# Sums of squares and roots of a query and key norm, with tokens on the partitions, and their order

## The reference

```
def rms_norm(x, g):
    xf = x.astype(jnp.float32)
    y = xf * lax.rsqrt(jnp.mean(xf * xf, axis=-1, keepdims=True) + NORM_EPS)
    return (y * g.astype(jnp.float32)).astype(x.dtype)
...
    q = q.reshape(B, T, H, 2, d)          # H = 4 heads, 2 components, d = 64
    k = k.reshape(B, T, H, 2, d)
    q = partial_rope(rms_norm(q, p['q_norm_g'])).astype(jnp.float32) * (d ** -0.5)
    k = partial_rope(rms_norm(k, p['k_norm_g'])).astype(jnp.float32)
```

## Time and profile before

| | |
|---|---|
| median of the runs | 2197.18 us |
| profiled execution, its own time | 2197.07 us |
| its span, first to last instruction | 2194.5 us |
| TensorE, matmuls | 1997.5 us (91%) |
| TensorE, weight loads | 1665.3 us (76%) |
| VectorE | 1411.1 us (64%) |
| ScalarE | 969.5 us (44%) |
| GpSimd | 349.1 us (16%) |
| granted TensorE clock, mean of the span | 0.950 |

### The profile page before, as it was taken

The page is one execution under the profiler, slowest core; times in us unless marked ns, Lnnn a source line. Parts: engine busy times, 40 slices in busy tenths (PEclk is TensorE's granted clock), DMA queues, the critical chain, the costliest instruction groups (busy, mean ns, idle before and its releaser), DMA issues. The chain is left out here.

```text
span 2194.5 us, 40752 instructions
## 1 busy us (share of the span) xinstructions
PE 1997.5 (91%) x16199; PEld 1665.3 (76%) x16199; DVE 1411.1 (64%) x2299; ACT 969.5 (44%) x1792; POOL 349.1 (16%) x354
## 2 busy tenths in 40 slices
PE   6999999997768888777999698899999999999999
PEld 4666777775545555576887387899999999988887
DVE  5877657674876667664777646656655565556666
ACT  7454467773744444443454322422232232333433
POOL 0000000000019993064454200000000000000000
PEclk8999999998879999958999899899999999999999
DMA  4111157777840001047884534022222222295343
GB/s 179 66 45 52 58 206 258 257 261 278 288 136 1 0 1 58 20 125 166 195 187 117 174 127 141 35 100 93 105 81 87 81 100 81 84 356 169 98 148 109
DMA packets 153305, 281.17 MB, mean 128 GB/s; under 512 B 13377, under 2 KB 85953, under 8 KB 150817
## 3 DMA queue, kind: packets, MB, share of 16 engines
q1 hardware_dynamic: 153120, 278.63, 39.8%
HBM read 172.53 MB, written 103.07 MB: 126 GB/s over the span
## 5 line engine op out<-in xcount | busy, mean ns | idle before, releaser
L2944 DVE TENSOR_TENSOR ff_lefts<-normed_raw,ff_lefts 128x512 fp32r<-128x512 f32 x154 | 105.5, 686 | 98.6 <-ACT ff_lefts L2828 98.6
L225 PE MATMUL ff_acc<-right_t_high,ff_lefts 128*128 128x320 f32 x528 | 163.1, 309 | 0.0
L224 PE MATMUL ff_acc<-right_t_low,ff_lefts 128*128 128x320 f32 x528 | 163.1, 309 | 0.0
L223 PE MATMUL ff_acc<-right_t_high,ff_lefts 128*128 128x320 f32 x528 | 163.1, 309 | 0.0
L223 PE MATMUL ff_acc<-normed_nl 128*128 128x512 f32 x385 | 149.8, 389 | 0.0
L225 PE MATMUL ff_acc<-normed_nl,normed_nh 128*128 128x512 f32 x385 | 149.8, 389 | 0.0
L2828 ACT CAST ff_lefts<-normed_raw 128x512 fp32r<-128x512 f32 x154 | 93.4, 620 | 116.2 <-DMA normed_raw<-in_w_up 56.1
L2854 ACT COPY normed_n<-ff_acc 128x640 f32<-128x640 f32 x66 | 45.9, 696 | 205.7 <-PE ff_acc L225 204.6
L1974 PE MATMUL at_pO<-heads_vt,at_amT 128*128 128x128 f32 (+1 forms) x624 | 104.6, 302 | 34.9 <-ACT at_amT L1918 24.5
L1974 PEld LDWEIGHTS at_pO<-heads_vt,at_amT 128*128 128x128 f32 (+1 forms) x624 | 82.8, 195 | 61.0 <-issue 40.0
L3016 DVE TENSOR_TENSOR normed_nl<-normed_raw,normed_nh 128x640 fp32r<-128x640 f32 x77 | 63.3, 822 | 91.7 <-ACT normed_nh L2877 91.7
(11 more groups left out here) (372 smaller groups left out, 5671.9 us busy)
## 6 DMA issues: line engine op xcount, KB each, us to landing
normed_raw<-dram_h SPq DMA_DIRECT2D x77, 320.0 KB, 3.0
ch_ops<-dram_sx SPq DMA_DIRECT2D x88, 256.0 KB, 5.2
dram_sx<-pr_sx SPq DMA_DIRECT2D x16, 1024.0 KB, 4.6
dram_h<-normed_spread_h SPq DMA_DIRECT2D x44, 320.0 KB, 2.3
pj_packed<-in_w_in SPq DMA_DIRECT2D x24, 512.0 KB, 4.9
heads_vt<-dram_ab SPq DMA_DIRECT2D x44, 256.0 KB, 5.4
normed_raw<-in_w_gate SPq DMA_DIRECT2D x22, 512.0 KB, 4.3
normed_raw<-in_w_up SPq DMA_DIRECT2D x22, 512.0 KB
```

Of the source, the lines that this page charges most:

```text
L223: nc.tensor.matmul(out, ll, rh, start=start, stop=False, skip_group_check=onto_kept)
L224: nc.tensor.matmul(out, lh, rl, start=False, stop=False, skip_group_check=onto_kept)
L225: return nc.tensor.matmul(out, lh, rh, start=False, stop=stop, skip_group_check=onto_kept)
L2944: tt(lefts[:, q % LEFTS, 1, :], raw[:, y, QUARTER[p], :], lefts[:, q % LEFTS, 0, :].bitcast(F32), ALU.subtract).then_inc(low, 1)
```

## The change

The sums are formed with the squares as weights: eleven blocks of 128 tokens, past each of which the two columns of `head_mean` move. The sums of token p of block w lie on partition p, columns 2w and 2w + 1: `st` is 128x22. ScalarE's root reads each of the 22 columns 64 times over (`by_rows`) and writes `rows`, 128x1408, tokens on the partitions. The spread takes each 128x128 block of `rows` as weights and the identity as the moving operand. `sq` is widened to 11 x 128 = 1408 columns, with the 96 at the end set to zero by GpSimd at the stage's start. `rows` has one buffer in place of two. The four `heads` matrices with their load, `quarter_mean` and the cuts at quarters and banks go.

The order changes too. TensorE does `sum_up(t+1)` ahead of `spread_roots(t)` and then the three `part`s; ScalarE does `root(t+1)` ahead of `square(t+2)`; VectorE does `inverse(t+1)` ahead of `scaled(t)`.

```
-        raw, sq0 = [g.raw_first, c.sb("raw1", (P, TOK))], c.sb("sq0", (P, TOK))
-        heads = c.sb("heads", (P, len(QUADS) * P))
+        raw, sq0 = [g.raw_first, c.sb("raw1", (P, TOK))], c.sb("sq0", (P, TT * P))
...
-        st = [c.sb(f"st{s}", (P, QTOK)) for s in range(2)]
-        rows = [c.sb(f"rows{s}", (P, QTOK)) for s in range(2)]
+        st = [c.sb(f"st{s}", (P, 2 * TT)) for s in range(2)]
+        rows = c.sb("rows", (P, TT * P))
...
-                sp.dma_start(heads[:, :], g.small_of("quarter_heads")).then_inc(small_in, 16)
...
             def _(pool):
+                for s in range(2):
+                    nc.gpsimd.memset(sq[s][:, TOK:TT * P], 0.0).then_inc(padded, 1)
                 sx_done(pool)
...
                     if t:
                         pe.wait_ge(meaned, t)
-                    for q, quad in enumerate(QUADS):
-                        last = nc.tensor.matmul(psq[quad, 0:QTOK], mean[:, :], sq[t % 2][:, q * QTOK:(q + 1) * QTOK], start=True, stop=True)
-                    last.then_inc(sums, 1)
+                    token_sums(nc, psq, sq[t % 2], mean[:, :]).then_inc(sums, 1)

                 def spread_roots(t):
                     pe.wait_ge(rooted, t + 1)
-                    if t == 0:
-                        pe.wait_ge(small_in, 16)
                     if t:
                         pe.wait_ge(roped, t)
-                    for lo, hi in zip(BANK_CUTS, BANK_CUTS[1:]):
-                        q = lo // QTOK
-                        last = nc.tensor.matmul(psn[:, lo:hi], heads[:, q * P:(q + 1) * P], rows[t % 2][:, lo - q * QTOK:hi - q * QTOK],
-                                                start=True, stop=True)
-                    last.then_inc(spreads, 1)
+                    spread(nc, psn, rows, ident, TOK).then_inc(spreads, 1)
...
                 for t in range(TILES - 1):
+                    sum_up(t + 1)
                     spread_roots(t)
-                    part(3 * t + 1)
-                    sum_up(t + 1)
-                    part(3 * t + 2)
-                    part(3 * t + 3)
+                    for n in range(3 * t + 1, 3 * t + 4):
+                        part(n)
...
                     act.wait_ge(inverted, t + 1)
-                    if t >= 2:
-                        act.wait_ge(spreads, t - 1)
-                    nc.scalar.activation(rows[t % 2][:, :], st[t % 2][:, :], ACT.Sqrt).then_inc(rooted, 1)
+                    if t:
+                        act.wait_ge(spreads, t)
+                    nc.scalar.activation(rows[:, :].rearrange("p (a n) -> p a n", n=HD), by_rows(st[t % 2][:, :], 2), ACT.Sqrt
+                                         ).then_inc(rooted, 1)
...
                     keep(3 * t + 1)
+                    root(t + 1)
                     if t + 2 < TILES:
                         square(t + 2)
-                    root(t + 1)
...
                 for t in range(TILES):
+                    if t + 1 < TILES:
+                        inverse(t + 1)
                     scaled(t)
                     if t + 1 < TILES:
                         with_sin(t + 1)
-                        inverse(t + 1)
                         with_cos(t + 1)
```

More of the change, by code:

```diff
@@ L87, in shape_constants @@
     out["centre"] = ((row[:, None] % HD == np.arange(HD)[None, :]) - 1 / HD).astype(np.float32)
[L88 to L92, removed]
     out["mean"] = np.full((P, 2), 1 / P, np.float32)
@@ L1006 @@
 QUADS = tuple(slice(BLK * q, BLK * (q + 1)) for q in range(P // BLK))
-QTOK = TOK // len(QUADS)
-BANK_CUTS = sorted({QTOK * q for q in range(len(QUADS) + 1)} | set(range(0, TOK, 512)))
 def steps_of(grp):
@@ L1528, in solve_and_attention_in @@
         two = lambda name, n=TOK: [c.sb(f"{name}{s}", (P, n)) for s in range(2)]
-        raw, sq0 = [g.raw_first, c.sb("raw1", (P, TOK))], c.sb("sq0", (P, TOK))
-        heads = c.sb("heads", (P, len(QUADS) * P))
-        mean, ident, swap, centre = (g.ahead_small[n] for n in ("quarter_mean", "ident", "swap", "centre"))
+        raw, sq0 = [g.raw_first, c.sb("raw1", (P, TOK))], c.sb("sq0", (P, TT * P))
+        mean, ident, swap, centre = (g.ahead_small[n] for n in ("head_mean", "ident", "swap", "centre"))
         swapped = c.sb("swapped", (P, 2))
-        st = [c.sb(f"st{s}", (P, QTOK)) for s in range(2)]
-        rows = [c.sb(f"rows{s}", (P, QTOK)) for s in range(2)]
+        st = [c.sb(f"st{s}", (P, 2 * TT)) for s in range(2)]
+        rows = c.sb("rows", (P, TT * P))
         swp = two("swp")
@@ L1538, in solve_and_attention_in @@
         cos, sin, v = g.cos_sb, g.sin_sb, g.v_rows
-        sq = [sq0, c.sb("sq1", (P, TOK))]
+        sq = [sq0, c.sb("sq1", (P, TT * P))]
         diag = [c.sb(f"diag{s}", (P, UNITS, BLK)) for s in range(2)]
@@ L1549, in solve_and_attention_in @@
             c.sem(n) for n in ("squared", "sums", "meaned", "rooted", "inverted", "spreads", "roped"))
-        small_in, blanked, swap_made, swap_kept = (
-            c.sem(n) for n in ("small_in", "blanked", "swap_made", "swap_kept"))
+        blanked, padded, swap_made, swap_kept = (c.sem(n) for n in ("blanked", "padded", "swap_made", "swap_kept"))
         sined, cosed, added = (c.sem(n) for n in ("sined", "cosed", "added"))
@@ L1725, in _ @@
                 pe.wait_ge(g.v_zeroed, 2)
+                pe.wait_ge(padded, 2)
                 turn_v(0)
@@ L1809, in inverse @@
                         dve.wait_ge(rooted, t - 1)
-                    nc.vector.tensor_scalar(st[t % 2][:, :], psq[:, 0:QTOK], 1e-6, None, ALU.add).then_inc(meaned, 1)
+                    nc.vector.tensor_scalar(st[t % 2][:, :], psq[:, 0:2 * TT], 1e-6, None, ALU.add).then_inc(meaned, 1)
                     dve.wait_ge(meaned, t + 1)
@@ L3108, in lend_ahead @@
         self.v_rows = [self.ahead.far(f"v{s}", (P, FT, 6 * CH)) for s in range(2)]
-        self.ahead_small = {n: self.ahead.far(n, (P, SCOLS[n][1])) for n in ("quarter_mean", "ident", "swap", "centre")}
+        self.ahead_small = {n: self.ahead.far(n, (P, SCOLS[n][1])) for n in ("head_mean", "ident", "swap", "centre")}
     def small_of(self, name):
```

## The result

The changed kernel takes 2235.3 us (median of 4 runs, 2231.06 to 2239.66) against 2194.31 before (median of 4 runs again, one of them the slow 3291.36 and the others 2189.88 to 2197.18): ratio 1.0188, 95% interval 1.0168 to 1.0208, 41 us slower. Forecast were 2226 and a range up to 2235. The direction, the ring and the size per tile came out. The forecast time is short by some 9 us and the forecast change, 28.8 us, by 12; the median lies 0.3 us above the range.

What follows compares the result with a forecast made beforehand. One stage was read as a ring of 10.5 us a tile, VectorE working through nearly all of it. A later first spread, six tiles of 15.0 us and a last round gave +28.8 us: 2226, range 2198 to 2235.

Steps and rivals of the forecast that it cites:

- the ring: Per tile, TensorE's sums wait for ScalarE's square, which waits behind a `keep` for a `part` behind spread and sums.
- Where the ring closes: From one spread's end to the next: 11.25 us at full clock, TensorE waiting 2.7 us or more for the square.
- Sums of two columns do not bring the clock back: After TensorE's wait the sums run at the low clock, 4.6 us (+2.2).
- VectorE leaves the path: Reciprocals shrink to about 0.29 us, VectorE's tile falls from 10.5 to about 8.3 us, 18 us in all.
- Rival 3: ScalarE sets the tile at 9.55 us, since waits do not add up in a ring; 2190 us, chance 0.13.
- the size of the sum: The whole stage's forecast change: +28.8 us, to 2226, what follows the stage being unchanged.
- The start: Stage's first tile: first sums 4.6 us, spread 4.0; first spread ends at 562.2, before at 552.88.
- The tile: 15.0 us for each of six tiles: 11.25 at full clock plus 3.75 for low clock in sums and spread.
- What follows is unchanged: After `turn_v(2)` starts at 661.5, before at 632.67, the rest of the kernel keeps its time.
- One wait for a store of `below`: ScalarE's two waits for these stores, 9.0 us together before, were taken to go with tiles of 15 us.
- rival 4: Spreading trains do not bring the clock back either, `part` low too: 16.6 us a tile, +38, 2235; chance 0.10.
- Rival 1: The sums bring the clock back like other work: 12.75 us a tile, +14.5, 2212 us; chance 0.22.

Runs made afterwards that it cites:

- run 7: Changed kernel with 128-column sums and three 512-column filler matmuls in TensorE's wait for the square; 2205.85 us, ratio 1.0043 to the kernel before.
- run 4: Changed kernel with 128 columns in place of two moving past each block of squares; 2218.53 us, ratio 1.0124 to the kernel before.
- run 6: Changed kernel's new forms in the order of before, with 128-column sums; 2204.12 us, ratio 1.0032 to the kernel before.
- run 9: New forms, order of before, 128-column sums, and SP's stores of `below` ahead of the round's loads; 2192.93 us, ratio 0.9995 to the kernel before.
- run 12: New forms, order of before, 128-column sums, stores of `below` first, root ahead of square in the second round; 2190.85 us, ratio 0.999.
- run 3: Changed kernel with ScalarE's square(t+2) moved ahead of keep(3t+1); 2216.86 us, ratio 1.0112 to the kernel before.
- run 1: Changed kernel's new forms, two-column sums, in the order of before on all three engines; 2206.5 us, ratio 1.0071 to the kernel before.
- run 8: Changed kernel, two-column sums, with three 512-column filler matmuls in TensorE's wait for the square; 2213.5 us, ratio 1.0097 to the kernel before.
- run 10: Kernel before, with only SP's stores of `below` moved ahead of the round's loads; 2190.26 us, ratio 0.9988.
- run 11: New forms, order of before, stores of `below` ahead of the round's loads, with two-column sums; 2207.52 us, ratio 1.0072 to the kernel before.

## Why the prediction was right or wrong

**What held.** *Where the ring closes*: TensorE's wait for the square was forecast at 2.7 us or more and is 3.40 in five rounds of seven (2.73 and 2.23 in the others); the other side of the ring is ScalarE's 41.7 us of waiting. At the full clock the ring was put at 11.25 us a tile; run 7 has 11.10. *Sums of two columns do not bring the clock back*: 3.95 to 4.86 us for the train against 4.6 forecast; runs 4 and 7 show it by taking it away. *VectorE leaves the path*: reciprocals of 0.29 us, root 1.38. *Rival 3* (ScalarE sets the tile) is what runs 6, 9 and 12 reach once order, clock and DMA waits allow it: in run 12 ScalarE works from one root to the same root a round later without a gap, in 9.39 and 9.38 us, against 9.55 reckoned. Single tiles are shorter (7.63 in run 3) where ScalarE's `keep`s of the round lag behind into the next.

**What failed is the size of the sum**, in three terms. The forecast for the stage was +28.8 us; in the profiled executions `turn_v(2)` moved from 632.67 to 669.84, of which 2.1 us had come about before the stage's first product (538.75 and 540.84): +35.1. The first product of the kernel before, then both products of the changed one:

```profile
538.75 0.58 PE L1724 MATMUL sa_psg<-all_par,ahead_swap 128*128 128x2 f32 x2 [12.50 <-DMA ahead_v<-dram_proj]
```

```profile
540.84 0.59 PE L1708 MATMUL sa_psg<-all_par,ahead_swap 128*128 128x2 f32 x2 [13.06 <-DMA ahead_v<-dram_proj]
...
669.84 3.01 PE L1705 MATMUL sa_banks<-ahead_centre,ahead_v 64*64 64x64 f32 x96 [0.59 <-ACT sa_below L1760]
```

1. *The start* (first spread ends at 562.2): it ends at 568.5, so 4.2 us too late with those 2.1 taken off. I took the first sums at the full clock, as in the earlier trace rows. In the changed kernel they stood behind a low `turn_v(0)` and took 4.85 us in place of 2.45, and the `turn_v` behind them 3.96 in place of 2.55 before, low too:

```profile
541.40:545.80 4.40, 4.40 (x81) 4.30 (x80) 0.16 (x1) 0.72 (x1) 0.00 (x0) 0.50 1.07 341
545.90:550.50 4.60, 4.60 (x22) 4.60 (x22) 0.00 (x0) 1.23 (x1) 0.00 (x0) 0.50 1.05 315
550.70:553.60 2.90, 2.90 (x56) 2.90 (x58) 2.78 (x4) 0.00 (x0) 0.00 (x0) 0.50 0.48 169
```

   The step that I applied to every tile, that the sums do not bring the clock back, I did not apply to the first train. In runs 1, 3 and 8 these first sums took 2.62, 2.89 and 2.62 us, with the same code ahead of them, so this term differs from execution to execution and its full size here is in part chance.
2. *The tile* (15.0): 15.3, six times, +2.0 us. The spread was taken at 4.0 us, with a full clock from 3.3 us on; in these tiles it is 4.16 to 4.88, 4.6 on average. Behind TensorE's wait the clock was low for some 3.3 us in the kernel before; in the tile shown it is low from 574.5 to about 584.4, through both trains.
3. *What follows is unchanged*: in this pair of executions the span after the stage grew by another 6 us, most of it in the chunk stage (189.3 us from its first to its last product from the state, 194.4 after). That stage took 189.5 to 193.7 us in the profiles of the twelve runs, and 191.6 in run 10, whose forms are those of before; so before and after lie at the ends of what it does anyway. Whether a part of it belongs to the change was not tried, and the cause of this term stays open.

One wait for a store of `below`, 2.1 us, stayed where I had put both at nothing; ScalarE waits 4.77 us for the next `part` behind it all the same, so it cost the ring nothing.

The 41 us of the medians are thus the stage's 35 and some 6 that it does not show. By luck rival 4 gave the measured number, 2235, by a mechanism that is half right: the spreads are nearly all low (its 4.5 us), but the `part`s are not, 2.67 to 2.96 us for three and only once 4.67, and its 16.6 us a tile did not occur. Rival 1's ground, that the clock is a matter of busy time, fails on run 1, where it fell with TensorE busy throughout.

The rule on weight loads in the Trainium skill ("TensorE: Matmul & The Clock Gate", section LDWEIGHTS) was weighed in the prediction: the estimate from it is 2.35 us for the sums at either clock. The trace decides against it for these forms: the 22 loads took 2.5 us at 1.00 (run 8) and 4.8 us at 0.50 (changed kernel). The same estimate holds for the spread, so that by the page the tile would have been shorter by 3.9 us and not by the 2.2 that I gave for the sums alone.

## What to carry to other kernels

Work that is moved ahead of another engine's turn must have its input ready one round before; draw the ring of waits with the new order and add up its sides at both clock levels before counting any engine's saved busy time. The train that moved 2 columns past 22 loads of weights was dear twice in this kernel: 2.6 us at the full clock where the old sums took 0.76, and the clock fell over it. With 128 columns in place of 2 it took 0.1 us more and the spreads behind it ran mostly at the full clock where no wait of several us stood ahead of them. Where a kernel has such a train, try it with more columns and read the granted clock behind it.

## What was not expected of the hardware

- More streaming made the kernel faster: 128 in place of 2 columns in the sums gave 14 us (run 4) and 17 us (run 9 against 11), though each train of sums was 0.1 us longer at the full clock (2.72 and 2.62) and 0.2 us longer at the low one.
- The clock fell from 1.00 to 0.50 with TensorE's busy time at 100% of the stretch (run 1, 572.0 to 577.5), over two-column sums; in run 3 it stayed at 0.50 for 23 us of unbroken work with such a train in it. In the busy time of the profile's page such a train looks like any other.
